# Where a branch's sum product and a chain of reductions stand in a sampled sparse-attention stage: moving one product into the next period's head, and one chain ahead of four page copies

## The reference, cut to what matters

```python
k_c = _compress(cmp_rows[:, :, 0], w1[0], b1[0], w2[0])
v_c = _compress(cmp_rows[:, :, 1], w1[1], b1[1], w2[1])
o_cmp, imp = _nsa_compressed(q, pos, k_c, v_c)
idx = _nsa_select(imp, pos, -(-L // SEL_BLOCK))
...
o_sel = _nsa_sel_attend(q_rot, pos, kg, vg, kpos)
...
o_win = _window_attend(q_rot, pos, keys[:, :, 0], keys[:, :, 1], kpos_w)
```

## Time and profile before

| | |
|---|---|
| median of 3 runs | 2726.25 us (2725.95 to 2731.45) |
| the profiled execution's own time | 2735.34 us |
| its span, first to last instruction | 2733.7 us |
| mean granted TensorE clock in it | 0.84 |
| PE, PEld busy | 2246.8 us (82%), 1672.6 us (61%) |
| DVE, ACT, POOL busy | 1320.9 us (48%), 729.2 us (27%), 302.7 us (11%) |
| DMA | 242.05 MB, mean 89 GB/s |

### The profile page before, as it was taken

The page is one execution under the profiler, slowest core; times in us unless marked ns, Lnnn a source line. Parts: engine busy times, 40 slices in busy tenths (PEclk is TensorE's granted clock), DMA queues, the critical chain, the costliest instruction groups (busy, mean ns, idle before and its releaser), DMA issues. The chain is left out here.

```text
span 2733.7 us, 35979 instructions
## 1 busy us (share of the span) xinstructions
PE 2246.8 (82%) x12280; PEld 1672.6 (61%) x12280; DVE 1320.9 (48%) x3088; ACT 729.2 (27%) x1512; POOL 302.7 (11%) x516
## 2 busy tenths in 40 slices
PE   6989657649967999997979896576499589999977
PEld 3544447637646888887345444576377468878863
DVE  1353476535535656564123434765355356566531
ACT  1120011114423444441212101111144234444302
POOL 0000000000032332320000000000000323324100
PEclk9999769756888999995979997697568889999859
DMA  4444010010055866662024430100100658768410
GB/s 145 149 143 119 10 34 1 2 47 1 1 131 141 182 160 148 147 134 62 21 102 145 146 116 10 34 1 2 47 1 1 136 132 183 168 143 187 107 70 35
DMA packets 176236, 242.05 MB, mean 89 GB/s; under 512 B 50406, under 2 KB 133126, under 8 KB 175372
## 3 DMA queue, kind: packets, MB, share of 16 engines
q1 hardware_dynamic: 151468, 172.51, 23.8%
q0 software_dynamic: 24576, 67.14, 10.5%
HBM read 223.17 MB, written 24.97 MB: 91 GB/s over the span
## 5 line engine op out<-in xcount | busy, mean ns | idle before, releaser
L588 PE MATMUL bank<-W,hT 128*128 128x512 f32 (+3 forms) x1152 | 447.8, 542 | 30.5 <-DMA W<-in_w_in 21.4
L1526 POOL DMA_DIRECT2D PC<-in_cache_nsa_kv x256 | 151.3, 591 | 2138.6 <-DVEq L195 1690.6
L588 PEld LDWEIGHTS bank<-W,hT 128*128 128x128 f32 x1152 | 218.6, 195 | 229.6 <-issue 183.1
L1212 PE MATMUL bank<-XT,W 128*128 128x256 f32 (+1 forms) x768 | 253.9, 466 | 0.0
L1194 PE MATMUL bank<-CF,RP 128*128 128x128 f32 x1024 | 152.4, 296 | 39.6 <-DVE RP L1182 37.7
L1201 ACT ACTIVATE XT<-bank 128x512 f32<-128x512 f32 x256 | 139.8, 593 | 165.7 <-PE bank L1194 165.7
L1212 PEld LDWEIGHTS bank<-XT,W 128*128 128x128 f32 x768 | 135.9, 191 | 50.9 <-issue 38.0
L1526 POOL DMA_DIRECT2D PS<-in_cache_nsa_kv x256 | 151.3, 591 | 141.2 <-issue 129.4
L1194 PEld LDWEIGHTS bank<-CF,RP 128*128 128x128 f32 x1024 | 123.6, 153 | 51.4 <-DVE RP L1182 40.9
L1730 PE MATMUL bank<-QBD,PS 128*128 128x64 f32 x1024 | 147.4, 294 | 0.0
L1730 PEld LDWEIGHTS bank<-QBD,PS 128*128 128x128 f32 x1024 | 146.2, 218 | 0.7
(11 more groups left out here) (378 smaller groups left out, 3709.6 us busy)
## 6 DMA issues: line engine op xcount, KB each, us to landing
PC<-in_cache_nsa_kv SPq DMA_DIRECT2D x256, 128.0 KB, 4.6
PC<-in_cache_nsa_kv POOLq DMA_DIRECT2D x256, 128.0 KB, 4.2
PS<-in_cache_nsa_kv POOLq DMA_DIRECT2D x256, 128.0 KB, 5.9
PS<-in_cache_nsa_kv SPq DMA_DIRECT2D x256, 128.0 KB, 6.3
W<-in_w_in SPq DMA_DIRECT2D x48, 512.0 KB, 4.5
XS<-scratch_conv_p SPq DMA_DIRECT2D x24, 384.0 KB
PW<-in_state_nsa_win SPq DMA_DIRECT2D x16, 512.0 KB, 3.8
Wo<-in_w_out SPq DMA_DIRECT2D x4, 2048.0 KB, 11.7
```

The source lines that it names most:

```text
L588: return nc.tensor.matmul(bk((c * NTILE + t) % 8)[:, 0:b - a], hT[:, k, t * P:(t + 1) * P], W[:, k // 2, k % 2, 0:b - a], start=(k == 0), ...
L1212: mm = nc_(self.v).tensor.matmul(out, self.v['W1'][:, kv, s, :], seg[:, s], start=(s == 0), stop=(s == SEG // PAIRS - 1))
L1526: e.dma_start(where[side * HD:(side + 1) * HD, slot, :, :], A['cache_nsa_kv'][l, page].rearrange("(p r) a g d -> p r (a g d)", r=PAIRS)[:, ...
```

## The change

The product over the selected branch's two sums (`sum_two`, name `ssb`) leaves the end of period p on PE and is made in period p + 1, behind `C1`; for the last sequence it is still made at the end. On VectorE, in the opening period alone, the four copies `R0.1` to `R3.1` go from ahead of the first compressed chain to behind the period's last operation (`A1`). In all other periods they stay. The lists of names follow.

```diff
@@ -1609,11 +1609,11 @@
         for j in range(8):
-            names_pe += at((f"kt{j+1} " if j < 7 else "") + f"ks{j}") + at({0: "C1"}.get(j, ""))
+            names_pe += at((f"kt{j+1} " if j < 7 else "") + f"ks{j}") + (at("C1") + pr("ssb") if j == 0 else [])
...
-            at("spq2") + co("H1 csb") + at("spv ssb")
+            at("spq2") + co("H1 csb") + at("spv") + ([f"ssb.{p}"] if p == last else [])
@@ -1621,8 +1621,8 @@
-        names_dve += at("wo0 wo1 snm ss0") + co("A0") + at("ss1 ss2 ss3") + co("C0") + nx("R0 R1 R2 R3") + \
-            co("cx0 cm cnd cnm cs0 cps") + at("sp0") + co("ccl crc pn pr0 pr1 A1") + at("sp1")
+        names_dve += at("wo0 wo1 snm ss0") + co("A0") + at("ss1 ss2 ss3") + co("C0") + (nx("R0 R1 R2 R3") if a else []) + \
+            co("cx0 cm cnd cnm cs0 cps") + at("sp0") + co("ccl crc pn pr0 pr1 A1") + at("sp1") + (nx("R0 R1 R2 R3") if not a else [])
@@ -1782,6 +1782,8 @@
                     if a and j == 0:
                         cb_.second(e, pe, act, dve, 1)
+                        if p > 0:
+                            sum_two(S_AT, b - 1)
@@ -1854,8 +1856,8 @@
                     values(f"spv.{b}", S_OUT, sel_v, SEL, 24, 2 * GT + 1)
-                    sum_two(S_AT, b)
-
+
+            sum_two(S_AT, last)
             turn_out(1, 3, "so1")
@@ -2013,7 +2015,8 @@
-                Rr(0, 4, q + 1)
+                if a:
+                    Rr(0, 4, q + 1)
@@ -2032,6 +2035,8 @@
                 if a:
                     sums("sp1", 0, 4, "se3", SEL + GT, NKEYG - GT, b)
+                if not a:
+                    Rr(0, 4, q + 1)
```

## The result

The changed kernel takes 2658.9 us in the median of four runs (2653.94 to 2664.56), the kernel before beside it 2726.1: ratio 0.9756, interval 0.9725 to 0.9787, 67 us less. The profiled execution took 2664.56 us at a clock of 0.856 (0.84 before).

A forecast was written before the change was run, and what follows sets the result against it. The prediction took PE's own instruction stream to bound the inner periods. Its terms, 20.4 + 24 + 11.4 + 14 = 69.8 us, off the profiled 2735.3 gave 2665.5, say 2666 us; range 2650 to 2706, the forecast's own 2650 to 2685.

The forecast's parts named there:

- The product (20.4 us): At 12 period boundaries, moving the product over the sums saves 1.7 us each, 20.4 us; ends 0 and 30.
- The charge of nothing for the fetch behind R4: In inner periods, SyncE's tile fetch after copy R4 would still land in time for VectorE's copy: 0 us charged.
- The 1.6 us of slack: Fetch of tiles 12 and 13: landing 3.3 us early, it keeps 1.6 us with the period 1.7 us ahead.
- The clock (24 us): In the twelve inner periods, without the pause PE's clock stays full: 24 us less; ends 0 and 24.
- the rival that the falls stay: Clock falls persist through the mask's wait or other light stretches: 33 us gained, 2693 us, chance 19%.
- The last periods (11.4 us): Last period of each layer: 1.7 us from the product plus 4 from the clock, twice, 11.4 us.
- May fall half way: In the last periods, PE's waits of 0.8 to 1 us may lower its clock: 4 taken of 7.7 us.
- The opening (14 us): Each layer's opening: PE's first transposes of the second sequence start earlier; 5.8 + 7.8, 14 us rounded; ends 0 and 20.
- the low clock's 7 us: Opening: PE starts out of a pause at low clock for some 7 us, costing 3 us per layer at 0.45 per us.
- the 1 us for the copies: Opening: the four moved copies follow their pages, costing the transposes behind the first copy 1 us.
- The 9 us between the profiled execution and the median: Whole kernel: profiled execution 9 us above the median 2726.25, put down to more clock falls, so forecast not shifted.
- The page's rule: At 12 boundaries, shared DMA engines bring selected pages no sooner: 0.5 us each, sum 6 us smaller, 2672 us.

The follow-up runs named there:

- the filled pause: Kernel before, with eight extra products of 64 columns, result unused, where PE waits for the second sum: 2700.88 us, ratio 0.9905.
- the kernel with the pause kept: Changed kernel, but PE waits for the second sum ahead of the next period's first key transposes: 2723.55 us, ratio 0.9985 to the kernel before.
- its repetition: The changed kernel with nothing altered, measured once more beside the kernel before: 2660.7 us, ratio 0.9739.
- the product alone: Changed kernel with the four copies back ahead of the first chain, only the product moved: 2682.95 us, ratio 0.9843 to the kernel before.
- the opening alone: Changed kernel with the product back at the period's end, only the four copies moved: 2718.55 us, ratio 0.9967 to the kernel before.

## Why the prediction was right, step by step

The time, 2658.9 us against 2666, lies in the range, and the sum, 69.8 us, stands beside 70.8 in the profiles. The two large terms, the product and the clock, are right in their mechanism; that the whole comes within 1 us is luck, as the smaller terms are off in both directions or vary from run to run.

- **The product (20.4 us):** right. 2.66 us is gone from each boundary, the mask product starts 7.94 us behind the transposes (7.9 forecast) and the period without falls is 50.90 (50.8 forecast), 1.6 less than 52.53. The charge of nothing for the fetch behind R4 came out right, but not as argued. The 1.6 us of slack was not there: in the period from 2251.34 on, SyncE issues this fetch 9.1 us behind the start, 3.0 us later than the 6.2 of before and not 1.7, it lands in 9.5 us and not 7.3, and VectorE's copy waits for it, which the prediction had as a sign of being wrong. What made it free, or nearly so, is that PE's transposes still find the copies done. The selected pages were not quite free: one boundary of each layer has 0.4 to 0.5 us more, for them.
- **The clock (24 us):** right, 23.3 by the filled pause. The mask's wait of 0.5 us did not trigger a fall, so the rival that the falls stay is out; the inner periods of the kernel with the pause kept are what it would have looked like.
- **The last periods (11.4 us):** the sum is right by chance. The stretches give 8.1 - 1.9 us, and the seventh boundary of each layer, which ends the opening's stretch, gives 2.66 each, 11.5 in all. "May fall half way" is not what happened: the clock fell 5.3 us behind the start in layer one and came back, and fell 2.2 us behind it in layer two and did not. In three profiles with the product in the head (the first, its repetition, the product alone) the six last periods take 51.5, 61.6, 58.3, 51.7, 58.9 and 58.8 us. Half of the gain fits their mean, 56.8, and none of them.
- **The opening (14 us):** under-sized. Of the 23.6 us in these two stretches 5.3 belong to the product, so 18.3 remain. The head start of PE's transposes came as forecast, from 10.26 to 0.49 us behind the first copy in layer one and from 10.89 to 0.49 in layer two, 9.8 and 10.4 us. What was taken off it was too much: 4 and 2.6 us forecast, 1.6 and 0.4 measured. The mis-sized terms are the low clock's 7 us (from PE's first transposes to the return of 1.00 it lasted 3.3 us in layer one and 4.0 in layer two, since the clock had fallen 3.0 and 2.4 us ahead of the copy) and the 1 us for the copies. At the prediction's own 0.45 per us, 3.3 us cost 1.5, and 4.0 us cost 1.8, less the 1.4 already paid 0.4: that is all of the measured price, and nothing is left for the copies. Where the low clock lasts for 17 us it costs 5 to 6 us more per layer, and the opening alone is then worth 8 us.
- **The 9 us between the profiled execution and the median:** the step of the text that the runs don't bear out. I took the difference for falls that the change removes. The changed kernel's own median is 6 us under its profiled execution, and both kernels spread widely: 2651 to 2670 us over 10 runs of the changed kernel, 2714 to 2751 over all runs of the one before, whose medians beside the experiments were 2724.6 to 2730.6. The 0.2% that I took a measurement to tell apart was too fine too: the intervals reach 0.3 to 0.4% to either side with 4 to 6 runs, and 0.2 to 0.3% with 12. The forecast against the median came out 7 us high for that and for the opening.
- **The page's rule.** With the Trainium skill's rule ("Trainium Kernel Development and Optimization", Key Constraints) that all queues share the same 16 DMA engines, the prediction had 2672 us. The late pages cost 0.5 and 0.4 us at one boundary of each layer, about 1 us in all, not 6.

The two parts alone give 43 and 8 us, 51, and together 67. Part of the gap is the opening's low clock, 5 to 6 us in each layer of the opening's profile; the intervals, 10 and 7 us to either side, can hold the rest, and it stays open.

## What to carry to other kernels

A short wait of TensorE that comes once per period can cost twice: its own time, and the clock behind it. Where a product waits for a late operand and its consumer is not urgent, put it behind work that is ready, and then count what stands behind the consumer on its engine, since the wait moves there, and the fetches that hang on it go out later. Read the clock's column period by period: equal instructions in periods of unequal length are the sign. One profile is one draw: the stretches that no edit touched differed by up to 17 us between two of them here, so read a part's gain in its own stretch and the whole in the medians.

## What was not expected of the hardware

- Eight useless products per boundary, 2 us each time, made the kernel before 25 us faster (0.9905), with the granted clock at 1.00 in every inner period.
- Behind the same wait, in the same program and execution, TensorE stayed at 1.2 GHz once for 17 us, where the clock had fallen 1.1 us ahead of the first page copy, and once for 7 us, where it had fallen 2.3 us ahead.
- Filler begun late did not hold the clock: 18 products started in the opening's wait at 1.00, the clock fell 1.5 us behind their start, and they took 6.61 us in place of 4.5.
- In one last period TensorE stayed at 1.2 GHz from 2.2 us behind the start to the end though it was busy for 53.46 of 61.60 us; in another execution of the same program the same period had the clock back after 6.8 us.
